# Expert layers of a two-block network: 24 instead of 16 tokens leave the dense first stage, and the search for picks starts three query tiles earlier

## The reference, cut to what matters

```
q  = (x @ w_q).reshape(t, 8, 2, 128)               # 8 heads, 2 halves
sc = einsum('thpc,hpnc->thpn', q, sub_keys)        # 128 scores per half
v_half, i_half = top_k(sc, 16)
cand     = v_half[:, :, 0, :, None] + v_half[:, :, 1, None, :]
cand_idx = i_half[:, :, 0, :, None] * 128 + i_half[:, :, 1, None, :]
top_s, pos = top_k(cand, 16)                       # 16 picks per head
expert = take_along_axis(cand_idx, pos)            # of 16384 experts
g   = softmax(top_s)
act = gelu(einsum('thkd,td->thk', u_tab[expert], x))
y   = einsum('thk,thkd->td', g * act, v_tab[expert])
```

## Time and profile before

| what | value |
|---|---|
| runs | 2003.53 us median of 3 (2002.76 to 2009.4) |
| profiled execution, its own time | 2015.55 us |
| span of the profiled execution | 2013.8 us |
| PE busy | 1953.6 us, 97% |
| DVE busy | 1642.4 us, 82% |
| ACT busy | 861.5 us, 43% |
| POOL busy | 427.5 us, 21% |
| read from HBM | 526.24 MB |

### The profile page before, as it was taken

The page is one execution under the profiler, slowest core; times in us unless marked ns, Lnnn a source line. Parts: engine busy times, 40 slices in busy tenths (PEclk is TensorE's granted clock), DMA queues, the critical chain, the costliest instruction groups (busy, mean ns, idle before and its releaser), DMA issues.

```text
span 2013.8 us, 35120 instructions
## 1 busy us (share of the span) xinstructions
PE 1953.6 (97%) x12472; PEld 1744.9 (87%) x12472; DVE 1642.4 (82%) x3458; ACT 861.5 (43%) x1663; POOL 427.5 (21%) x340
## 2 busy tenths in 40 slices
PE   7999999989999989999999999999999899999998
PEld 6888887868999989988888787899999899888886
DVE  6899886866798469789999977669964995999998
ACT  6557544555210100056565665541111002655566
POOL 0000000000135543312114200002455341211350
PEclk9999999989999999999999999999999999999999
DMA  6545335506599999977789964257999997777996
GB/s 247 221 167 198 116 108 154 185 10 206 196 361 408 410 390 336 327 248 245 247 282 366 336 197 145 65 188 291 405 408 410 353 341 267 255 258 243 324 390 216
DMA packets 136870, 529.72 MB, mean 263 GB/s; under 512 B 14748, under 2 KB 14876, under 8 KB 134080
## 3 DMA queue, kind: packets, MB, share of 16 engines
q1 hardware_dynamic: 93760, 376.33, 53.0%
q0 software_dynamic: 43008, 152.10, 20.0%
HBM read 526.24 MB, written 1.05 MB: 262 GB/s over the span
## 4 chain that ended last, share of the span: by engine, by line
PE 65%; DVE 9%; DMA 5%; issue 4%; POOL 3%; ACT 2%; SPq 0%; DVEq 0%; ACTq 0%
PE bank L2508 24%; PE bank L347 9%; PE bank L348 9%; PE bank L349 9%; PE bank L2539 4%; PE bank L2540 4%; POOL e_gbuf L2317 3%; DMA wbuf<-in_peer_v 3%; PE bank L2380 3%; DVE x_tok L2337 2%; DMA e_gbuf<-in_peer_rows,e_row_at 2%; DVE tile_lo L2892 1%; DVE tile_lo L277 1%; PE bank L2465 1%; DVE w_parts L2895 1%
## 5 line engine op out<-in xcount | busy, mean ns | idle before, releaser
L2508 PE MATMUL bank<-h_dense,wbuf 128*128 128x176 f32 x4096 | 632.2, 315 | 2.5 <-issue 2.3
L2508 PEld LDWEIGHTS bank<-h_dense,wbuf 128*128 128x128 f32 x4096 | 614.3, 191 | 4.0 <-issue 3.4
L2654 ACT ACTIVATE tile_hi<-wbuf 128x1024 fp32r<-128x1024 f32 x248 | 263.4, 1062 | 232.1 <-PE bank L349 126.9
L2892 DVE TENSOR_TENSOR tile_lo<-wbuf,tile_hi 128x1024 fp32r<-128x1024 f32 x256 | 313.0, 1223 | 28.3 <-ACT tile_hi L2617 15.9
L2317 POOL DMA_INDIRECT e_gbuf<-in_peer_v,e_row_at x128 | 210.2, 1642 | 533.1 <-DVE x_tok L2337 498.9
L2628 ACT ACTIVATE e_hidden<-bank 128x352 f32<-128x352 f32 x128 | 59.4, 464 | 577.7 <-PE bank L2508 535.9
L2331 DVE CUSTOM_DVE_ANT_0 e_gbuf<-e_gbuf,x_gathered 128x1024 f32<-128x1024 f32 x128 | 156.1, 1227 | 80.2 <-DMA e_gbuf<-in_peer_rows,e_row_at 80.0
L2317 POOL DMA_INDIRECT e_gbuf<-in_peer_rows,e_row_at x128 | 162.6, 1270 | 237.7 <-issue 110.2
L2539 PE MATMUL bank<-tile_hi,w_parts 128*128 128x512 f32 x512 | 206.5, 403 | 0.5
L277 DVE TENSOR_TENSOR tile_lo<-wbuf,tile_hi 128x1024 fp32r<-128x1024 f32 (+2 forms) x117 | 140.5, 1212 | 73.9 <-ACT tile_hi L269 72.9
L2540 PE MATMUL bank<-tile_lo,w_parts 128*128 128x512 f32 x512 | 199.8, 390 | 0.0
(11 more groups left out here) (412 smaller groups left out, 3584.4 us busy)
## 6 DMA issues: line engine op xcount, KB each, us to landing
wbuf<-in_peer_u SPq DMA_DIRECT2D x128, 1024.0 KB
wbuf<-in_peer_v SPq DMA_DIRECT2D x256, 512.0 KB
wbuf<-in_w_in SPq DMA_DIRECT2D x16, 2048.0 KB, 7.8
wbuf<-in_peer_q SPq DMA_DIRECT2D x32, 512.0 KB
wbuf<-in_hyb_in SPq DMA_DIRECT2D x16, 512.0 KB
wbuf<-in_mla_uq SPq DMA_DIRECT2D x9, 512.0 KB
wbuf<-in_mla_in SPq DMA_DIRECT2D x8, 528.0 KB
wbuf<-in_w_v SPq DMA_DIRECT2D x2, 2048.0 KB, 7.3
```

The costliest lines, as they stand in the source:

```text
L2508: last = nc.tensor.matmul(bank[:, j // 2 % 2, j % 2 * S + EXTRA:j % 2 * S + DENSE], deep[:, slot, k * P:(k + 1) * P], h_dense[:, k, PLAIN] ...
L2654: nc.scalar.activation(tile_hi[:, slot, 0:D], ring[:, slot, 0:D], ACT.Copy).then_inc(hi_done, 1)
L2892: nc.vector.tensor_tensor(tile_lo[:, slot, 0:D], ring[:, slot, 0:D], tile_hi[:, slot, 0:D].bitcast(F32), ALU.subtract).then_inc(lo_done, 1)
```

## The change

`BLOCKS` gets a second block of 8 tokens, so `EXTRA` is 24, `DOTS` 88 and `ITEMS` 152, and the dense first stage has 168 columns instead of 176. `EARLY` is 16 instead of 8. The first two groups of scores come after the ninth query tile (`SCORES_AT` = 8). VectorE's rests of the last four query tiles are made at the first four places of the first half search, and in the second half search the first 8 items' dots are made. The places of items and of ScalarE's waits are moved.

```
-BLOCKS = ((0, 16),)
+BLOCKS = ((0, 16), (16, 8))
-    EARLY = GBUFS
+    EARLY = 2 * GBUFS
-    TAKEN, LAST_TAKE = (28, 36, 46, 64, 96, 108), 122
-    EXPS_AT, FEW_AT = (10, 25), 28
-    ACTS_AT, ACTS = 45, (slice(0, 48), slice(48, SHARED))
+    TAKEN, LAST_TAKE = (34, 42, 50, 60, 93, 109), 123
+    EXPS_AT, FEW_AT = (11, 26), 31
+    ACTS_AT, ACTS = 52, (slice(0, 48), slice(48, SHARED))
-    SCORES_AT, SOON = 11, 2
+    SCORES_AT, SOON = 8, 2
 # tensor
-            if j == 6:
+            if j == 4:
                 pe.wait_ge(xn_done, NT)
                 turn_normed(0)
-            if j == 9:
+            if j == 6:
                 pe.wait_ge(h_done, 4)
                 turn_normed(4)
             if j == SCORES_AT:
                 pe.wait_ge(h_done, KT)
+                pe.wait_ge(q_kept, 4)
                 pe.wait_ge(keys_loaded, DMA)
 # scalar: dense_columns(0) at j == 5 (was 7), dense_columns(4) at j == 7 (was 10)
 # vector
-        for j in range(HALVES - 1):
+        for j in range(SCORES_AT):
...
-        dve.wait_ge(lo_done, M_U)
-        dve.sem_inc(lo_done, NKEYS)
...
+        def last_rests():
+            nonlocal chances
+            if SCORES_AT + SLOTS + chances < HALVES:
+                rest_tile(nc, dve, g, M_Q + SCORES_AT + SLOTS + chances)
+            chances += 1
+        def first_dots():
+            nonlocal chances
+            chances += 1
+            take(min(max(0, chances - 4) * 8 // 12, GBUFS))
         for half in range(2):
             dve.wait_ge(sc_kept[1], (1, 3)[half])
-            find_picks(1, slice(PH // 2 * half, PH // 2 * half + PH // 2), lambda: None)
+            find_picks(1, slice(PH // 2 * half, PH // 2 * half + PH // 2), (last_rests, first_dots)[half])
+            chances = 0
+            if half == 0:
+                dve.wait_ge(lo_done, M_U)
+                dve.sem_inc(lo_done, NKEYS)
...
-            take(chances * TAKEN[0] // 27)
+            take(GBUFS + chances * (TAKEN[0] - GBUFS) // 27)
```

More of the change, by code:

```diff
@@ L2585, in scalar @@
         for j in range(HALVES):
+            if j == 5:
+                dense_columns(0)
             if j == 7:
-                dense_columns(0)
-            if j == 10:
                 dense_columns(4)
@@ L2841, in vector @@
                                                op0=ALU.mult, op1=ALU.add).then_inc(rows_ready, 1)
+            if half == 0:
+                dve.wait_ge(rows_ready, 5)
         nc.vector.scalar_tensor_tensor(out=row_of_few[FEW, :], in0=pick[FEW, 1, 0, :], scalar=float(NKEYS), in1=pick[FEW, 1, 1, :],
@@ L2844, in vector @@
         dve.wait_ge(rows_ready, 8)
-        chances = 0
         def sometimes():
```

## The result

The changed kernel takes 1993.49 us (median of 17 runs, 1987.89 to 2000.76), the kernel before 2007.15 us (median of 17 runs beside them, 2002.43 to 2017.94). The ratio is 0.992, with a 95% interval of 0.9906 to 0.9933: faster by 0.8%, some 16 us by the ratio and 14 us by the medians. Forecast were 22 us and a time of 1981 us in a range of 1967 to 1997, against a kernel before of 2003.53 us; beside the changed kernel that one took 2007.15. The profiled execution after took 1989.47 us, its span is 1987.7 us.

A forecast was written before the change was run, and what follows sets the result against it. It took TensorE's column-bound products to bound the way to key 80, a late gather there, then VectorE. Terms summed to -11.1 us a layer, -22.2 for two, from 2003.5 to 1981 us; range 1967 to 1997.

The forecast's parts named there:

- late U: Rival, before key 80: U lands at only 2.49 us a key, key 80 comes 6.6 us late; 1991 us, chance 0.14.
- dear second stage: Rival, second stage: tiles at 2.65 us because V lands later, +7.6 us more a layer; 1996 us, chance 0.14.
- the wait at key 80: TensorE's wait for gathers falls from 6.5 to about 1.3 us; with the key after it, -6.5 us a layer.
- The narrower products: First stage: eight fewer columns save 6.5 ns an instruction, -8.3 us before key 80 and -5.0 after it.
- ScalarE at pair 31: First stage: moved dots land near 679 us, TensorE is held only past 689, so no cost.
- U on its reserve: Before key 80: TensorE wants U at 230 GB/s and gets 211 while gathers are queued; +1.5 us a layer.
- The weighing: After key 80: VectorE just keeps up, so the products save their 5.0 us; +1.0 jitter, +0.4 small matmuls.
- the slow key: Key after a layer's first weights, 3.80 us instead of 2.39, partly at the lower clock; should mostly go.
- The second stage: V tiles with 59 items instead of 48: +0.5 us to tile 71, then 2.50 us a tile, +5.3.
- The rival on the other side: Slower: moved dots land at 708 us, too late for ScalarE at pair 31; 2019 us, chance 0.07.
- Nothing given back: Rival: the second stage's items fit into existing jitter and U keeps up, -19.3 us a layer; 1965 us, chance 0.14.
- At no cost: Moved scores, their new wait, the last query tiles' rests, 16 more vector DMAs and SP's later U loads cost nothing.

The follow-up runs named there:

- columns alone: Kernel before with 24 few tokens instead of 16, its search left where it was, eight items first: 2013.52 us, ratio 1.0026.
- narrow alone: Kernel before with products of 168 columns, hidden values of tokens 16 to 23 left out, no gathers or moves added: 2000.67 us, ratio 0.9961.
- search alone: Changed kernel with 16 few tokens instead of 24, keeping the early search and sixteen items first: 1997.75 us, ratio 0.9942 to the kernel before.
- again: The changed kernel once more, no edit: 1992.88 us, ratio 0.9929 to the kernel before.
- moves early: Changed kernel with the second few-token block's row numbers moved eight items earlier: 1984.68 us, ratio 0.988 to the kernel before.
- values fewer: Changed kernel without the last eight values (weighted sums) of each layer: 1986.43 us, ratio 0.988 to the kernel before.
- split moves: Changed kernel with row numbers moved eight items earlier and finished dots moved block by block: 1986.95 us, ratio 0.9901 to the kernel before.
- both: Changed kernel with row numbers moved eight items earlier and twice the descriptor room: 1984.28 us, ratio 0.9885 to the kernel before.

## Why the prediction was right and where it failed

The sign and the range held. 22 us were forecast and 14 to 16 came, at 1993.5 us and not 1981, nearer to the times of the rivals "late U" and "dear second stage" than to the forecast's own, though neither rival's mechanism came about. The range held in part by luck: the largest step but one, the wait at key 80, gave 0.3 us of 5.2, and two other rows were better than forecast (-8.9 for -6.8, +3.8 for +5.3). The steps, one by one:

**The narrower products: right.** With nothing else in the way, 1280 of them take 182.50 us, where those of 176 columns take 191.04: 142.6 and 149.3 ns each, 6.7 ns saved (forecast 6.5), -8.5 us. Columns set the time. The row reads -8.9, since the kernel before lost 0.9 us in the mean over its own 191.04.

**The wait at key 80: the step that failed.** The prediction had item 60 land some 6 us before key 80, and the wait fall from 6.5 to 1.3 us. It is 4.92 us in the first layer, and from the turn to the first weights it is 8.2 us in the mean, before 8.4. The start was too high as well: 6.5 us was the largest of the four waits before (3.99 to 6.49), and of the 8.4 us only 4.3 could go, for no kernel here gets under 4.16. What I reckoned well is the beginning and the goal: the first gather goes out at 530.49, which is 535.3 by the start that I had (forecast 535), and key 80 is reached in 183 us. What I mis-sized is POOL. "Some 10 us in which nothing lands" should have been 17. POOL's timeline in the kernel after:

```profile
562.75 3.94 POOL L2302 DMA_DIRECT2D e_row_few<-e_stage  x8 [0.84 <-DVE e_stage L2862]
579.19 1.30 POOL L2317 DMA_INDIRECT e_gbuf<-in_peer_rows,e_row_few  x1 [12.49 <-DMA e_row_few<-e_stage]
...
618.21 1.54 POOL L2302 DMA_DIRECT2D e_row_few<-e_stage  x3 [0.68 <-issue]
631.16 1.00 POOL L2317 DMA_INDIRECT e_gbuf<-in_peer_rows,e_row_few  x1 [11.41 <-DMA e_row_few<-e_stage]
...
661.30 2.05 POOL L2308 DMA_DIRECT2D e_stage<-e_dots_few  x4 [0.94 <-issue]
...
677.44 1.62 POOL L2317 DMA_INDIRECT e_gbuf<-in_peer_rows,e_row_at  x1 [2.00 <-issue]
684.53 0.96 POOL L2317 DMA_INDIRECT e_gbuf<-in_peer_rows,e_row_at  x1 [5.47 <-issue]
```

I took 4.40 us for the landing of moved row numbers, from the earlier trace rows. There the eight small DMAs had followed 16 us of waiting with hardly a gather left. Now gathers are queued ahead of them, since dots free their buffers during the search, and it takes 12.49 and 11.41 us, twice in a layer, and no gather is issued meanwhile. In the first layer this first landing takes 3.0 to 4.7 us in the four profiles with the old search (before twice, columns alone, narrow alone) and 11.2 to 12.5 us in the eight with the early one. The dots' 24 moves are the third pause; POOL issues one gather at 677.44 and the next at 684.53 only. The queues (packets, MB, share), in 620 to 650 and in 660 to 700, show what is lost:

```profile
q0 software_dynamic: 1592, 3.94, 35.6%
...
q1 hardware_dynamic: 2378, 9.15, 58.6%
q0 software_dynamic: 2581, 6.61, 43.7%
```

At the 199 GB/s of the earlier trace rows the gathers (q0) would have had 5.97 and 7.96 MB in the two stretches: 2.03 and 1.35 MB are missing, which is 10.2 and 6.8 us, 17 in all, 7 more than forecast. The first pause's landing cost another 8.1 us (12.49 for 4.40), of which the search gave back 2.5: its moves went out at 562.75, where I had 570 less the 4.8 us by which this layer starts earlier. So the forecast's 709, which is 704 by this start, becomes 704 + 7 + 5.6 = 717; the last of the 60 dots starts at 714.50. Key 80 was forecast for 717.4 less 4.8 = 712.6 and came at 711.94. The experiments show the cause. With the second block's row numbers moved early and nothing else changed the wait is gone (4.17 us from the turn to the weights, 1.07 of them idle). Search alone, which has no second block, agrees: its memset starts 184.9 us after the layer's first product with 64 items dotted, that of the kernel after 187.5 us with 60. The right row for the landing was in the profile of before all the same: a gather needs 18.05 us among eight, and landings behind eight gathers (10 us and more) are how I priced ScalarE at pair 31, while I priced the pause at 4.40. The queue was the same in both.

**U on its reserve: +1.5, measured under +0.5 (183.0 against 182.5), and not independent of the step above.** Of that 0.5 the wait for U is 0.4 us in one layer of the four ("again", at pair 10); 0.9 us in another is ScalarE, see below. U was saved by the pauses that made the gathers late. When moves early takes one pause away, the turn slips to 184.6 and 186.2; narrow alone, with one pause, to 188.7. So the rival "late U" stands right behind the wait for gathers: while both queues have work, here in 700 to 714 us, U (q1) and the gathers (q0) get as many packets,

```profile
q1 hardware_dynamic: 771, 2.96, 52.7%
q0 software_dynamic: 772, 2.81, 50.1%
```

and what one wins the other loses. The Trainium skill, DMA: Bandwidth & Descriptors, section Queues, rings and completion order, has a DMA engine take a packet from each queue with work in turn; these rows agree. Late U is why repairing the failed step gives 4 us a layer and not the 6 that the wait and what follows it cost (4.0 and 1.9).

**The weighing: right.** -4.9 us, where the forecast had -3.6 without the slow key. The jitter of 1.0 that I added didn't come, and the slow key's 1.3 did not go (4.08 us in the first layer, before 3.80); the two errors nearly cancel. With the early moves, where TensorE hardly idles at key 80, it takes 124.6 us, another 1.9 less: a mean granted clock of 1.00 there against 0.98 after, so the lower clock that follows the idle time at key 80 has its price in this row.

**The second stage: right in kind, too dear.** Tiles 0 to 71 cost +0.4 (+0.5). Tile 72 to the end costs +3.8 (+5.3). VectorE is the bound, as worked out: 120.98 of 122.26 us, 99%. In the same stretch `L2910` and `L2337` (the rests and the items) and then the chief wait:

```profile
1023.16:1145.42 122.26, 61.04 (x51) 1.00 0.97 372
...
1023.16:1145.42 122.26, 53.74 (x43) 1.00 0.97 372
...
ACT tile_hi L2655 <- DMA wbuf<-in_peer_v: 45.6, 44, 3.2
```

VectorE takes 2.45 us a tile counted over 50, where I forecast 2.50 with most of the old surplus of 0.13 put on top of its 2.41. The old surplus did not stay on top: VectorE idles for 1.28 us in 50 tiles. The four values of each kernel spread by 2 to 4 us there, so +3.8 is good to about 1 us; values fewer puts the price of eight items at 2.9.

**ScalarE at pair 31: priced at nothing, and it met the limit.** ScalarE waited until 683.79. With the layer's start 4.8 us earlier my landing at 679 is 674 and the limit at 689 is 684: it landed on the limit.

```profile
683.79 0.31 ACT L2637 ACTIVATE e_stage<-e_stage 24x128 f32<-24x128 f32 x1 [8.70 <-DMA e_stage<-e_dots_few]
```

TensorE was held there once, at 684.48:

```profile
684.48 27.63 PE L2509 MATMUL bank<-h_dense,wbuf 128*128 128x168 f32 x192 [0.76 <-ACT e_hidden L2629]
```

That pair of keys starts 0.9 us late, which is most of the first layer's 183.53 over 182.50. The rival on the other side stayed away, but the ten us of margin that I had reckoned were gone. In the second layer ScalarE waited for 5.9 us and cost nothing. Split moves, which cut this wait to 1.7 us, ran no faster for it.

**The rivals.** Late U did not decide, and is what comes next. Nothing given back is out: 3.8 us a layer are. A dear second stage is out at 2.45 us a tile. The slower side is out with a landing at 683.8, where by this layer's start it decides from 695 on.

**At no cost.** The scores, rests and dots in the search show no price: the layer's first product starts at 528.41 and 530.11, before at 533.23 and 532.89, and search alone reads 4.2 us at key 80 and 629.4 us a layer (before 636.0). The earlier start is no gain of the change either: narrow alone and columns alone, with the old search, start at 527.75 and 529.76.

**What would show it.** Shown: products of 143 ns, the weighing near 126 us, VectorE above 95% (98 to 100), no wait at pairs 31 to 33 over 1 us, and the first gather near 535 (530.49, with a start that is 4.8 us earlier). Not shown: the first weights after 188 to 190 us (measured 189.9 to 192.2, one of four inside), tiles at 2.50 us (2.43 to 2.47).

So the change wins because the search and the first items come earlier; the narrower products are paid out only through that. The version with the early moves is faster than both kernels by its own run: 1984.7 us, 0.988 (0.9856 to 0.9903) against 0.992 (0.9906 to 0.9933) for the change, each to the kernel before on its own chip. Of the two kernels that build on it, both repeats it (0.9885, up to 0.9906) and split moves is at 0.9901, whose interval overlaps that of the change.

## What to carry to other kernels

Price a small DMA that an engine waits for by what is queued ahead of it at that moment after the change, not by its time before: 4.40 us became 12. A pause in one queue is the other queue's gain, so look who lives on the pauses before you close them. And when two halves of a change free time on both sides of one meeting point, time the halves alone: one gave 6.6 us a layer, the other 0.3, for the meeting point waits for the later side.

## What the runs showed of the hardware that was not expected

Small DMAs issued behind queued gathers kept POOL for 11.4 to 12.5 us until they had landed, in this kernel (11.41, 12.49) and in the first layer of the others with the early search (11.2 to 13.2), against 3.0 to 4.7 us with few gathers queued (4.40 in the earlier trace rows).

POOL's issue of a gather takes 0.94 us or up to 1.56 us and more; with twice the descriptor room the mean in 640 to 711 us fell from 1.26 to 1.03 us and the idle time put down to "issue" from 22.4 to 3.7 us. So in the changed kernel a part of POOL's time goes to waiting for room and not to its work. Twice the room moved the wait to the buffers, which are no sooner free.

Between the two expert layers, in code that the change doesn't touch, two of the twelve profiles are some 8 us longer. The stretch from 1168 to 1298 us in the second profile of the kernel before has a granted clock of 0.92, where the kernel after has 1.00:

```profile
1168.00:1298.00 130.00, 124.38 (x687) 109.95 (x688) 87.26 (x169) 72.48 (x154) 0.00 (x0) 0.92 0.35 109
```

```profile
1168.00:1298.00 130.00, 124.92 (x741) 108.26 (x740) 92.45 (x181) 79.54 (x166) 0.00 (x0) 1.00 0.39 123
```

The way from the last product of one layer to the first of the next was 202.38 us there and 202.41 us in columns alone, and 192.9 to 195.9 us in the other kernels. The same stretch of columns alone has a granted clock of 0.92 as well. Over whole executions its mean granted clock is 0.978 to 0.986 in twelve runs, and 0.983 to 0.993 in the nineteen of the kernel before beside them. So a part of the spread of the runs, and of columns alone's 1.0026, is not its layers. What sets this clock off was not found.
